# Gathering the next expert's tokens mid-expert and combining rows one expert late

## What is computed

```python
logits = xf @ w_router
top_logits, top_idx = lax.top_k(logits, 2)
gates = softmax(top_logits)
# for each expert e, the tokens that chose it (a block holds up to 128 rows):
xb = xf[tok]                                   # gather
hb = silu(xb @ w_gate[e]) * (xb @ w_up[e])     # 1024 -> 3584
yb = hb @ w_down[e]                            # 3584 -> 1024
out[tok] += yb * gate                          # combine
x = x + out
```

## Time and profile before

| | us |
|---|---|
| median of 3 runs | 3363.33 |
| lowest, highest | 3363.05, 3369.65 |
| span of the profiled execution | 3364.6 |
| PE busy in that span | 3046.8 (91%) |
| DVE busy | 2052.4 (61%) |
| ACT busy | 1575.3 (47%) |
| the experts, first `gate_up` to last `down` | 545.9 to 1605.1 |

### The profile page before, as it was taken

One profiled execution on the slowest core, in us unless ns is written; L12 is line 12 of the kernel. 1 busy time (PEld: TensorE's weight loads), 2 busy tenths in 40 slices (PEclk: granted clock), 3 DMA queues, 4 the chain that ended last, 5 costly groups with the idle time before them and its releaser, 6 DMA issues.

```text
span 3364.6 us, 50875 instructions
## 1 busy us (share of the span) xinstructions
PE 3046.8 (91%) x19949; PEld 2706.0 (80%) x19949; DVE 2052.4 (61%) x2278; ACT 1575.3 (47%) x1796; POOL 39.6 (1%) x99
## 2 busy tenths in 40 slices
PE   7799978999999999999999967879999997798799
PEld 7499867988988989989898946747989895495598
DVE  5645556787887887888555555444555447543554
ACT  5344345676776766767443422124434343312442
POOL 4000000000000000000000000000000000000000
PEclk9799988999999999999999957889999997588899
DMA  6155535999999999999455400024545542002253
GB/s 217 50 175 187 171 129 180 360 318 310 360 316 305 358 311 349 321 316 361 151 187 163 148 24 13 1 77 136 187 163 184 178 152 70 13 1 67 75 186 136
DMA packets 475067, 623.01 MB, mean 185 GB/s; under 512 B 16512, under 2 KB 424464, under 8 KB 474960
## 3 DMA queue, kind: packets, MB, share of 16 engines
q1 hardware_dynamic: 471008, 618.08, 54.8%
q10 hardware_dynamic: 2352, 3.37, 0.3%
q0 software_dynamic: 1600, 0.10, 0.0%
HBM read 620.45 MB, written 1.05 MB: 185 GB/s over the span
## 4 chain that ended last, share of the span: by engine, by line
PE 85%; DVE 7%; ACT 4%; issue 3%; ACTq 0%; DMA 0%; DVEq 0%; POOL 0%; POOLq 0%
PE banks L697 20%; PE banks L760 19%; PE banks L719 10%; PE banks L790 9%; PE banks L640 8%; PE banks L670 4%; PE banks L579 2%; DVE pT L1692 1%; PE banks L827 1%; PE banks L1106 1%; PE banks L1093 1%; PE banks L1105 1%; PE banks L651 1%; PE banks L853 1%; PE banks L1066 1%
## 5 line engine op out<-in xcount | busy, mean ns | idle before, releaser
L2029 DVE TENSOR_TENSOR w_low<-ring,w_up 128x2048 fp32r<-128x2048 f32 x336 | 765.0, 2290 | 158.6 <-ACT w_up L1422 72.1
L1422 ACT ACTIVATE w_up<-ring 128x2048 fp32r<-128x2048 f32 x336 | 638.8, 1917 | 103.4 <-DMA ring<-in_moe_w_up_dram 81.8
L1795 DVE TENSOR_TENSOR w_low<-ring,w_up 128x2048 fp32r<-128x2048 f32 x174 | 393.7, 2288 | 436.5 <-PE banks L719 427.8
L1242 ACT ACTIVATE w_up<-ring 128x2048 fp32r<-128x2048 f32 x174 | 325.8, 1906 | 0.0
L1246 ACT ACTIVATE sg<-banks 128x256 f32<-128x256 f32 x116 | 44.5, 384 | 590.3 <-PE banks L697 590.3
L760 PE MATMUL banks<-w_up,hT_up 128*128 128x256 f32 x1792 | 256.2, 285 | 21.5 <-DVE hT_low L2060 21.5
L697 PE MATMUL banks<-hT_up,w_up 128*128 128x256 f32 x1856 | 267.6, 286 | 6.8 <-ACT hT_up L1196 6.8
L760 PEld LDWEIGHTS banks<-w_up,hT_up 128*128 128x128 f32 x1792 | 239.0, 191 | 35.2 <-issue 24.0
L697 PEld LDWEIGHTS banks<-hT_up,w_up 128*128 128x128 f32 x1856 | 249.4, 191 | 21.4 <-ACT hT_up L1196 10.2
L697 PE MATMUL banks<-hT_low,w_up 128*128 128x256 f32 x1856 | 261.0, 284 | 0.0
L697 PE MATMUL banks<-hT_up,w_low 128*128 128x256 f32 x1856 | 260.7, 283 | 0.0
(11 more groups left out here) (401 smaller groups left out, 4484.2 us busy)
## 6 DMA issues: line engine op xcount, KB each, us to landing
ring<-in_moe_w_gate_dram SPq DMA_DIRECT2D x112, 1024.0 KB, 5.2
ring<-in_moe_w_up_dram SPq DMA_DIRECT2D x112, 1024.0 KB, 5.4
ring<-in_moe_w_down_dram SPq DMA_DIRECT2D x112, 1024.0 KB, 5.0
ring<-in_ffn_w_in_dram SPq DMA_DIRECT2D x88, 1024.0 KB, 5.1
ring<-in_ffn_w_out_dram SPq DMA_DIRECT2D x44, 1024.0 KB, 5.0
ring<-in_mix_w_in_dram SPq DMA_DIRECT2D x26, 1024.0 KB, 5.3
ring<-in_ffn_w_gate_dram SPq DMA_DIRECT2D x14, 1024.0 KB, 5.1
ring<-in_ffn_w_up_dram SPq DMA_DIRECT2D x14, 1024.0 KB, 5.1
```

What stands on the lines that cost most here:

```text
L1242: f(w_up[:, s, :], ring[:, s, :], ACT.Copy).then_inc(sem["hi_ready"], 1)
L1422: f(w_up[:, s, :], ring[:, s, :], ACT.Copy).then_inc(w.sem["hi_ready"], 1)
L1795: v.tensor_tensor(w_low[:, j, :], ring[:, s, :], w_up[:, s, :].bitcast(F32), ALU.subtract).then_inc(sem["lo_ready"], 1)
L2029: v.tensor_tensor(w_low[:, i % NLOW, :], ring[:, s, :], w_up[:, s, :].bitcast(F32), ALU.subtract).then_inc(w.sem["lo_ready"], 1)
```

## The change

Each expert now owns one half of the activation tiles `hT_up` and `hT_low`: even experts columns 0 to 127, odd experts 128 to 255 (`mine`). `selT` has two copies, one for each half. The pieces of work are moved as follows.

- PE: `gather` for the next expert stands between `step(11)` and `step(12)` of the present one, and writes `acc[2]`, `acc[3]`. The transposes of `selg` (`turn_gates`) stand between `step(12)` and `step(13)`; they use `acc[2]` and so wait for `chosen_h_ready`. The combine of an expert is done in the next one, in two parts: token tile 0 after `turn_hidden(0)`, token tile 1 after `step(2)`, both in `acc[2]`, `acc[3]`. `gate_up(0)` waits for nothing but its weights.
- DVE: the additions to `x` follow `step(1)` and `step(2)`, `select` for the next expert follows them, and the two subtractions that make `hT_low` (`chosen`) follow `step(12)`. They are now 2 operations on 128x512 in place of 8 on 128x128.
- ACT: the copy to `ye` stands in `step(0)` of the next expert, `chosen` (2 operations on 128x512 in place of 8) in `step(12)` ahead of `silu(12)`, and the copy to `selT` in `step(13)`.
- The scale by `norm_ffn` is taken out of the gather's path: before the experts DVE multiplies `xn` once by a row table `gain_row` (2 operations on 128x1024), which ACT's queue loads (0.5 MB) after the recurrent part.
- The loop holds two experts and runs three times. The first and the last expert are written out.

```diff
-                gate_up(0)
-                gate_up(1, up_slot(0))
-                turn_hidden(0, up_slot(1))
-                pe.wait_ge(sem["expert_added"], w.next("expert_added"))
-                for t in range(TT):
-                    ins = turn(acc[2][:, t * P:t * P + P], selg[:, t, :])
-                ins.then_inc(sem["selT_psum"], 1)
-                step(2)
-                step(3)
...
+                def turn_gates():
+
+                    pe.wait_ge(sem["chosen_h_ready"], w.next("chosen_h_ready", 2))
+                    for t in range(TT):
+                        ins = turn(acc[2][:, t * P:t * P + P], selg[:, t, :])
+                    ins.then_inc(sem["selT_psum"], 1)
+
+                def combine(t, whose, freed=None):
+
+                    if t == 0:
+                        pe.wait_ge(sem["selT_ready"], w.next("selT_ready"))
+                        pe.wait_ge(sem["expert_out"], w.next("expert_out"))
+                    else:
+                        pe.wait_ge(sem["expert_added"], w.next("expert_added"))
...
+                def expert(mine, first=False, last=False):
...
+                    gate_up(0, mine, None if first else last_slot)
+                    gate_up(1, mine, up_slot(0))
+                    turn_hidden(0, up_slot(1))
+                    if not first:
+                        combine(0, 1 - mine)
+                    step(2)
+                    if not first:
+                        combine(1, 1 - mine)
+                    step(3)
+                    with w.loop(n // 2 - 3, {"lo_ready": 6, "hidden_ready": 2, "hidT_ready": 2}):
+                        step(4)
+                        step(5)
+                    if not last:
+                        if not first:
+                            pe.wait_ge(sem["expert_added"], w.next("expert_added"))
+                        gather()
+                    step(n - 2)
+                    if not last:
+                        turn_gates()
+                    step(n - 1)
+                    turn_hidden(n - 1)
+                    down(n - 2)
+                    down(n - 1, last=True)
...
+                    step(n - 3)
+                    step(n - 2)
+                    if following is not None:
+                        chosen(1 - mine)
                     step(n - 1)
                     lower(expert_loads(n + 1)[0])
                     hidden_lower(n - 1)
```

More of the change, by code:

```diff
@@ L808, in expert_ffn, with gather @@
-                ins.then_inc(sem["selT_psum"], 1)
-                step(2)
-                step(3)
-                with w.loop(n // 2 - 2, {"lo_ready": 6, "hidden_ready": 2, "hidT_ready": 2}):
-                    step(4)
-                    step(5)
-                turn_hidden(n - 1)
-                down(n - 2)
-                down(n - 1, last=True)
+                def gather():
+                    pe.wait_ge(sem["sel_ready"], w.next("sel_ready"))
+                    for c in range(DC):
+                        for t in range(TT):
+                            ins = mm(acc[2 + c // 4][:, (c % 4) * P:(c % 4) * P + P],
+                                     xn[:, t, c * P:c * P + P], sel[:, t, :],
+                                     start=(t == 0), stop=(t == TT - 1))
+                        if c % 4 == 3:
+                            ins.then_inc(sem["chosen_h_psum"], 1)
@@ new lines, in expert, with step @@
+                def expert(mine, first=False, last=False):
+                    def step(k):
+                        gate_up(k, mine)
+                        turn_hidden(k - 1, up_slot(k))
+                        down(k - 2, first=(k == 2))
+                    gate_up(0, mine, None if first else last_slot)
[21 more added lines that the diff above has]
+                    down(n - 1, last=True)
@@ L818, in attention @@
+                return gather, turn_gates, combine, expert, last_slot
             def attention(units):
@@ L927, in experts @@
             def experts(w, slots):
-                def gather():
-                    pe.wait_ge(sem["sel_ready"], w.next("sel_ready"))
-                    for c in range(DC):
-                        for t in range(TT):
-                            ins = mm(tr[c // 4][:, (c % 4) * P:(c % 4) * P + P],
-                                     xn[:, t, c * P:c * P + P], sel[:, t, :],
-                                     start=(t == 0), stop=(t == TT - 1))
-                        if c % 4 == 3:
-                            ins.then_inc(sem["chosen_h_psum"], 1)
@@ L939, in expert @@
-                def expert(last=False):
-                    pe.wait_ge(sem["chosen_h_ready"], w.next("chosen_h_ready", 2))
-                    expert_ffn(w, slots)
-                    if not last:
-                        gather()
-                    pe.wait_ge(sem["selT_ready"], w.next("selT_ready"))
-                    pe.wait_ge(sem["expert_out"], w.next("expert_out"))
-                    for t in range(TT):
-                        for h in range(2):
-                            ins = mm(ebank[2 * t + h][:, :], selT[:, t, :],
-                                     ye[:, h * HALF:h * HALF + HALF], start=True, stop=True)
-                    ins.then_inc(sem["expert_psum"], 1)
@@ L953, in experts @@
-                gather()
-                per = {"lo_ready": 42, "hidden_ready": 14, "hidT_ready": 14, "sel_ready": 1, "selT_ready": 1,
-                       "chosen_h_ready": 2, "expert_out": 1, "expert_added": 1}
-                with w.loop(N_EXP - 1, per):
-                    expert()
-                expert(last=True)
-                w.next("expert_added")
+                gather, turn_gates, combine, expert, last_slot = expert_ffn(w, slots)
+                gather()
+                turn_gates()
@@ new lines, in experts @@
+                expert(0, first=True)
+                per = {"lo_ready": 84, "hidden_ready": 28, "hidT_ready": 28, "sel_ready": 2, "selT_ready": 2,
+                       "chosen_h_ready": 4, "expert_out": 2, "expert_added": 4}
+                with w.loop(N_EXP // 2 - 1, per):
+                    expert(1)
+                    expert(0)
+                expert(1, last=True)
+                pe.wait_ge(sem["expert_added"], w.next("expert_added"))
+                combine(0, 1, last_slot)
+                combine(1, 1)
@@ L1437, in step @@
                         upper(first + 1)
+                    if then is not None:
+                        then()
                     silu(k)
@@ L1981, in _ @@
             finish_h(lambda c: col("ffn", DC + c))
+            dve.wait_ge(sem["inputs_loaded"], w.next("inputs_loaded", 16))
+            for t in range(TT):
+                v.tensor_tensor(xn[:, t, :], xn[:, t, :], gain_row[:, :], ALU.mult)
             dve.wait_ge(sem["logits_psum"], w.next("logits_psum"))
@@ L2072, in rest @@
                     hidden_lower(n - 1)
-                return start, rest
+                    if following is not None:
+                        lower(0)
+                        lower(1)
+                return lower, chosen, add, expert
             def experts(w, slots):
-                start, rest = expert_ffn(w, slots)
+                lower, chosen, add, expert = expert_ffn(w, slots)
                 def select(e):
```

148 lines of the change are left out of this document (83 added, 65 removed).

## The result

The changed kernel takes 3371.64 us (median of 20 runs, 3366.31 to 3377.47). In the same rounds the kernel before takes 3365.54 us (20 runs, 3361.76 to 3370.64). The ratio is 1.0018, with a 95% interval of 1.0011 to 1.0024: 6 us slower. That is clear of the noise, and 0.18% lies within the 0.2% that the forecast took as the same, though the upper end of the interval doesn't. 3368.3 was forecast, with a range of 3357 to 3375. Of the 3.3 us that the time lies higher, 2.2 are the kernel before, whose median over 20 runs is higher than over the three runs that the forecast started from.

A forecast was written before the change was run, and what follows sets the result against it. PE's own work was taken to bound the steps, leaving gains only at expert boundaries. 3364.6 - 20.2 + 23.8 + 1.7 - 0.7 + 0.2 = 3369.4, brought to the median 3368.1, plus 0.2 for the branch: 3368.3 us, range 3357 to 3375.

The forecast's parts named there:

- the middle case ("the same"): Outcome within 0.2% of no change, a time from 3356.6 to 3370.1 us; given 0.53, slower 0.38, faster 0.09.
- The removed wait: At expert boundaries, PE's wait for DVE's hT_low before the first gate_up goes: 2.89 us seven times, -20.2 us.
- The added wait: In step(12), PE's selg transposes wait for subtractions queued behind the lower of d11: 3.4 us seven times, +23.8 us.
- points (2) and (3): Signs: seven PE waits of about 3.4 us at selg's transposes, released by hT_low, each after a lower awaiting PE's down.
- The clock: Behind the seven new waits, PE's clock falls five times instead of four, 8.5 us against 6.8: +1.7 us.
- Its rival, a fall behind every wait: Clock falls behind six or seven of the new waits instead of five, giving 3370.0 to 3371.7 us; chance 0.22.
- Gather, combine and DVE's debt at no cost: Moved gather and combine wait for nothing; DVE's 4.1 us of additions and selection in steps 1 and 2 are covered.
- point (6): Sign in the changed kernel's profile: combines without a wait.
- The start of expert 0: Before the first gate_up, fewer ACT and DVE operations gain half a microsecond, and moved transposes 0.2: -0.7 us.
- The loop's branch: PE's branch back shows 0.09 us, taken twice: 0.2 in all. Rival: exposed up to 2.74 each, 5.5 in all; chance 0.1.
- The tail: Behind the last expert, combine and additions in turns in two banks, three hand-overs in place of one: +0.2 us.
- Not there: the wait: Rival: DVE finishes the two subtractions before down(10) ends, so no new wait or clock falls: 3336.0 us; chance 0.08.

The follow-up runs named there:

- e1: Changed kernel with DVE's two subtractions into hT_low moved two loads up, behind the lower of g13 instead of d11; 3341.6 us, ratio 0.9935.
- e4: Kernel before, order untouched, with only the gain taken out of the gather's path and 2 larger operations for 8 small ones; 3354.33 us, ratio 0.9972.
- e5: Changed kernel with two extra scratch multiplications on DVE ahead of the two subtractions, lengthening each wait of PE; 3396.51 us, ratio 1.0092.
- e6: Changed kernel with e1's early subtractions and e2's written-out loop together; 3336.36 us, ratio 0.991.
- e2: Changed kernel with the loop of three passes over two experts written out on PE, ACT and DVE; 3369.38 us, ratio 1.0012.
- e3: Changed kernel with the body of the second pass over the experts left out on all engines, test and branch kept; 3366.55 us, ratio 1.0006.
- e9: Changed kernel without PE's wait for the last addition ahead of the branch over the second pass; 3371.26 us, ratio 1.002.

## Why the prediction was right, and where it was not

The time fell in the range and in the middle case ("the same"), by a thin margin. The forecast named 3370.1 as the time from which a change could be told, and 3371.6 is above it; the ratio stays under 1.002 because the kernel before came out 2.2 us higher over 20 runs than over three, which is luck. By the steps of the prediction:

- **The removed wait, -20.2.** Right, and a little small. In the kernel before an undisturbed expert was 132.58, in e1 it is 129.53: 3.05 each, 21.4 in all. No `gate_up` of an expert's start waits for `hT_low` any more. Point (1) asked for no idle time there at all; that holds for five of the seven, and ahead of experts 3 and 5 PE stood for 1.5 and 1.7 (the branch, below).
- **The added wait, +23.8.** Right in its place, its releaser and its size, points (2) and (3): seven of 3.16 to 3.19 us of idle time, each behind a `lower` that waited 0.53 to 0.58 for PE's `down`. The subtractions take 1.28 together, 1.3 was taken. From start to start one costs 3.38, 3.4 was forecast. The undisturbed expert is 132.92, with 133.1 forecast in point (4).
- **The clock, +1.7.** Too high by a fall: four and not five, 7.3 us in place of 6.8, so +0.5. It fell behind the seven waits and nowhere else, point (5). The reason given for five, that a longer wait drops the clock more often, isn't borne out between 1.86 and 3.2 us: four of seven in e4 at 1.86, four of seven before at 2.7, two to four of seven in four profiles at 3.17. Only e5's 5.43 brought all seven. Its rival, a fall behind every wait, did not occur in any profile with the wait of 3.17; how many falls the other executions had isn't known.
- **Gather, combine and DVE's debt at no cost.** Right, point (6): there is no wait at a combine inside the experts, and PE's window in e6 has no gap at all.
- **The start of expert 0, -0.7.** Too small. From gather to `gate_up` 1.4 were gained, and another 1.5 because the clock was up when `gate_up` began (1.00 against 0.72). e4, which has only this part and the shorter scaling, shows it without the rest.
- **The loop's branch, +0.2.** This step failed. It took from the earlier trace rows that the branch "shows with 0.09", and from the inner loop that branches leave no gap. Both rows were read rightly, but they are of branches with a short way back; over a body of two experts it took 4.7 to 4.9 us, and 1.5 to 1.8 of it showed, twice: 3.6 us start to start (1.81 each by the distances 134.73 and 137.44). The section of the Trainium skill that the rival's part cites said so, and the rival was given 0.1. Nor was it so that no row of the trace showed such a stall: the kernel before has a branch of 5.19 us at 2480.0, back over a whole layer, and one of 5.28 at 1607.3, forward over the second pass, both in PE's sequencer records and both hidden. Queued matmuls cover 3.65 us of the first, which leaves an estimate of 1.5 for each of the two branches of the loop; that is what showed. e2, where the branches and the gaps go together, bears the rival out, and its ceiling of 5.5 held.
- **The tail, +0.2.** This step failed, and it is the largest error: +5.8. Of it, e3 gives 4.8 to the skipped second pass, on PE and on DVE, and leaves 1.0 for the hand-overs; by the four other kernels with the same skipped body the second pass is 3.3 to 3.6, and the rest goes with a dearer branch (4.72) in the changed kernel's profile, for a reason that isn't known. The prediction counted hand-overs of semaphores, and overlooked that the added wait on PE stood ahead of a branch that the combine and the additions had hidden (5.28 us from 1607.3 in the kernel before).
- **Not there: the wait.** This rival (3336.0) didn't occur, because of the order on DVE that the prediction named. Where e1 and e6 change that order, 3341.6 and 3336.4 were measured.

**The sum again**, from the gather of expert 0 to the last `down`: before 1604.51 - 536.88 = 1067.6, after 1606.42 - 535.49 = 1070.9, so +3.3. The terms as measured: -21.4 + 23.7 + 0.5 + 3.6 - 2.9 = +3.5. Then the tail, 5.8: +9.1 in all, against +5.0 in the forecast. (The forecast takes 1.3 off a span to come to a median, which mixes two measures; it cancels, since the result is 3363.3 + 5.0 either way.) The excess of 4.1 shows in the medians as 1.1 only (6.1 us between them, 5.0 forecast): the profiled execution of after lay 3.9 above its median, at one of the lower mean clocks (0.917, where the six at 0.920 were the fastest as a group) and with the dearer branch in the tail. The right result thus rests on the two large terms, which nearly cancel and were right. Of the small ones, the branch and the tail were 3.4 and 5.6 too low, the start, the clock and the removed wait 2.2, 1.2 and 1.2 too high; that these errors cancel in part is luck.

**Open**: why the clock falls behind some of the waits of 1.9 to 3.2 us and not behind others (2 of 7 in e2, 4 of 7 in the changed kernel, e3, e4 and e9, and in e3 other ones of the seven than in the changed kernel); what sets a PE branch's price between 3.3 and 5.5 us, over one and the same body too (3.33 to 4.72); and whether the tail's gain in e9 is real in the median.

## What to carry to other kernels

Before moving a step, look at what stands in front of its result on the engine that makes it: a result that is queued behind work which itself waits for the consumer's last step comes late for the next one, and two lines moved on the producer (e1, 30 us under the changed kernel) were worth more here than the whole change of order. A wait that is added ahead of a branch or a register load can expose all that these had done unseen; count the branch with its full length in the sequencer's records and not with the gap it used to leave. Look for a branch's price in the trace of before, in all of the kernel and not only where the change is. When a profile names an engine as the releaser that had been done before the wait ended, look into the waiting engine's own queue.

## What the runs showed of the hardware

- PE's compare-and-branch took 0.07 to 0.23 us in the experts' loops with a body of up to one expert, 4.6 to 5.0 us back over a body of two experts, 5.2 back over a whole layer (before), and 3.3 to 5.5 us forward over the skipped second pass (3.33, 3.33, 3.58, 3.74, 3.82, 4.72, 4.80, 5.28, 5.50, 5.52 in ten kernels, 4.80 and 5.52 over the short body); over an empty one 0.21. ACT's and DVE's took 0.04 to 0.07 in the same places, but DVE stood idle for 2.5 to 2.7 us behind the branch over the long body, and 0.28 behind the one over the short body.
- PE can hide some 3.3 us of such a branch behind matmuls that it has queued: the branch at 935.3 took 4.73, and 1.51 of it showed.
- The granted clock fell behind four of seven waits of 1.86 us, four of seven of 2.7, two to four of seven of 3.17, and seven of seven of 5.43, at 1.3 to 2.7 us each, and in e1 behind one of two waits of 1.5 to 1.8. Each count is from one profiled execution.
